# Moving the convolution, the fourth head's logits and the layer norm around TensorE's queue in a one-layer encoder block

## What is computed

```python
h = rms_norm(x, g_mix)
u_conv, q, k, v, qi, ki, wi, gc, ga = split(h @ w_in)
# conv branch
a, gate = split(u_conv, 2)
v = a * sigmoid(gate)                       # 512 channels
v = depthwise_causal_conv(v, 31 taps) + conv_b
y_conv = silu(layer_norm(v, ln_g, ln_b)) @ w_conv_out
# attention branch: 8 heads, 2 groups of keys, keys chosen by an indexer (top 128)
y_attn = softmax(q k / 8 + rel_bias, chosen keys only) v @ w_attn_out
x = x + (sigmoid(gc) * y_conv + sigmoid(ga) * y_attn) @ w_out
```

## Time and profile before

| | |
|---|---|
| runs | 720.65, 720.75, 723.16 us; median 720.75 |
| profiled execution | 723.9 us, span 722.1 us |
| mean granted TensorE clock | 0.91 |
| TensorE busy | 566.6 us (78%) |
| VectorE busy | 353.0 us (49%) |
| ScalarE busy | 258.5 us (36%) |
| POOL busy | 249.9 us (35%) |

### The profile page before, as it was taken

How to read it: one execution, slowest core, us unless ns; L and a number is a source line. 1 busy time by engine, 2 the same in 40 slices (tenths; PEclk the granted TensorE clock), 3 DMA queues, 4 the chain that set the end, 5 groups by cost and what they waited for, 6 DMA issues and landing times.

```text
span 722.1 us, 12345 instructions
## 1 busy us (share of the span) xinstructions
PE 566.6 (78%) x4247; PEld 377.3 (52%) x4250; DVE 353.0 (49%) x740; ACT 258.5 (36%) x443; POOL 249.9 (35%) x434
## 2 busy tenths in 40 slices
PE   3899999964979997989999903889988959696810
PEld 3577788742646564557788802445444524353400
DVE  4329999987887765186913282121212111111136
ACT  6344432312334465476431400323333322232312
POOL 5332444311212121124653005334453542434314
PEclk9999999985979999899999955999999999999965
DMA  8213532420120203023316698999999999999653
GB/s 281 62 60 94 199 93 83 117 58 0 59 59 1 58 1 117 10 108 116 106 41 233 224 414 331 380 408 407 361 347 408 409 408 408 408 403 398 242 224 130
DMA packets 58812, 149.21 MB, mean 207 GB/s; under 512 B 8660, under 2 KB 25044, under 8 KB 58782
## 3 DMA queue, kind: packets, MB, share of 16 engines
q1 hardware_dynamic: 53438, 139.89, 51.8%
q0 software_dynamic: 5200, 8.41, 3.2%
q10 hardware_dynamic: 144, 0.52, 0.2%
HBM read 145.37 MB, written 12.08 MB: 218 GB/s over the span
## 4 chain that ended last, share of the span: by engine, by line
PE 42%; DVE 28%; SPq 12%; issue 6%; DMA 6%; ACT 4%; POOL 1%; DVEq 1%; ACTq 0%; POOLq 0%
PE bank L650 20%; PE bank L871 9%; SPq L407 9%; DVE bank L1214 7%; PE bank L888 5%; DVE bm L1192 4%; DVE m L1191 4%; SPq L417 3%; DMA region<-in_w_e_up 2%; DVE conv_buf L1183 2%; PE bank L722 2%; PE bank L848 2%; PE bank L753 1%; ACT region L1015 1%; PE bank L819 1%
## 5 line engine op out<-in xcount | busy, mean ns | idle before, releaser
L524 POOL TENSOR_TENSOR w_part<-region,w_part 128x1024 fp32r<-128x1024 f32 (+1 forms) x52 | 110.1, 2117 | 246.5 <-ACT w_part L922 246.5
L650 PE MATMUL bank<-h_hi,w_part 128*128 128x512 f32 (+1 forms) x528 | 174.1, 405 | 3.2 <-DVE h_lo L1141 1.7
L650 PEld LDWEIGHTS bank<-h_hi,w_part 128*128 128x128 f32 (+1 forms) x528 | 100.7, 191 | 34.8 <-issue 9.1
L871 PE MATMUL bank<-region,kT 128*32 128x256 f32 x1536 | 93.5, 398 | 16.6 <-DMA region<-in_w_e_up 12.2
L650 PE MATMUL bank<-h_lo,w_part 128*128 128x512 f32 (+1 forms) x264 | 105.4, 399 | 0.0
L1477 DVE TENSOR_TENSOR mask_b<-mask_b,bank 128x128 f32<-128x128 f32 x30 | 8.6, 288 | 188.0 <-ACT mask_b L1100 117.8
L1214 DVE SCALAR_TENSOR_TENSOR bank<-glu,cv,bank 128x512 f32<-128x512 f32 x116 | 87.6, 755 | 19.0 <-DVE bank L1214 14.0
L871 PEld LDWEIGHTS bank<-region,kT 128*32 128x32 f32 x1536 | 56.0, 115 | 61.5 <-issue 39.1
L922 ACT ACTIVATE w_part<-region 128x1024 fp32r<-128x1024 f32 (+1 forms) x52 | 48.0, 924 | 107.2 <-PE bank L650 107.1
L550 POOL TENSOR_TENSOR carrier<-mhalf 128x1 f32<-128x1 f32 x184 | 32.9, 196 | 125.7 <-ACT qT L1104 117.0
L650 PEld LDWEIGHTS bank<-h_lo,w_part 128*128 128x128 f32 (+1 forms) x264 | 50.6, 192 | 11.0 <-issue 0.7
(11 more groups left out here) (252 smaller groups left out, 807.1 us busy)
## 6 DMA issues: line engine op xcount, KB each, us to landing
region<-in_w_e_down SPq DMA_DIRECT2D x22, 1024.0 KB
region<-in_w_e_gate SPq DMA_DIRECT2D x44, 512.0 KB
region<-in_w_e_up SPq DMA_DIRECT2D x44, 512.0 KB
region<-in_w_in SPq DMA_DIRECT2D x16, 1024.0 KB, 6.0
gates<-in_w_e_gate SPq DMA_DIRECT2D x20, 512.0 KB
gates<-in_w_e_up SPq DMA_DIRECT2D x20, 512.0 KB
conv_buf<-in_w_e_down SPq DMA_DIRECT2D x10, 1024.0 KB
region<-in_w_out SPq DMA_DIRECT2D x2, 2048.0 KB, 7.7
```

The lines of the kernel that those rows point to most:

```text
L524: g.tensor_tensor(unit_part(u, 1), unit_raw(u), unit_part(u, 0).bitcast(F32), ALU.subtract)\
L650: last = mm(out_, a_parts[p], b_parts[q], start=start and x_ == 0, stop=stop and x_ == 2)
L871: last = mm(bank[0][32 * c:32 * c + 32, 0:FF], xTs[:, k, at_:at_ + 32], w_gu[slot][:, e, :, half, k, j * P:(j + 1) * P], start=(half == 0 ...
```

## The change

It has four parts.
1. The convolution: each tap becomes two instructions of 256 columns, the two halves in turns; a half waits for the same half of the tap before. All 248 are written out, with no rolled loop. A table says how many taps stand where: first ahead of the reciprocal of a round, then between the logits of three heads and those of the fourth; 12 are left for behind the last round.
2. In each round the logits of the next round's fourth head move behind the value product on TensorE, and behind the second piece of taps on VectorE. The output copy of a round moves from the next round into its own.
3. The attention branch (units 33 to 40) moves ahead of the layer norm, of which the channel mean, the variance and the spreading stand between its units. `o_part` gets another layout, so that its first half can be written while the last round still uses its probabilities. Branch products use banks 2, 3, 4, 0.
4. The variance becomes one number per token (16 products with one column of ones), POOL raises it to the power -1/2 between two weight splits, VectorE scales an identity by it, and one product with ones spreads it over the partitions. The square root, the reciprocal and the correcting steps go.

```diff
-        o_part = part("o_part", [P, 2, CC, T], r0_at + 4 * 4096)
+        o_part = part("o_part", [P, CC, 2, T], r0_at + 4 * 4096).rearrange("p c u n -> p u c n")
...
             for u in range(NUNIT):
                 split_lo(u)
+                if u == AO0 + 5:
+                    pool.wait_ge(S["lnvar_ready"], 1)
+                    g.tensor_tensor(rs[:, 2, :], ss[:, 2, :], mhalf[:].to_broadcast([P, TB]), ALU.pow)\
+                        .then_inc(S["lnstd_ready"], 1)
...
                 project(units_a[i])
-                if i + 1 < len(attn):
-                    logits(i + 1, (3,))
...
                 last.then_inc(S["pv_mm"], 1)
-                if i == len(attn) - 1:
...
+                if i + 1 < len(attn):
+                    logits(i + 1, (3,))
                 if units_b[i]:
                     project(units_b[i])
...
+            def channel_variance():
+
+                pe.wait_ge(S["sq_ready"], CC)
+                for b in range(TB):
+                    for c in range(CC):
+                        last = mm(bank[7][:, b:b + 1], sT[:, c, b * P:(b + 1) * P], ones[:, 0:1],
+                                  start=(c == 0), stop=(c == CC - 1))
+                last.then_inc(S["ln_mm"], 1)
+
+            def spread_rstd():
+
+                pe.wait_ge(S["diag_ready"], 1)
+                mm(bank[7][:], ones[:], score, start=True, stop=True).then_inc(S["ln_mm"], 1)
...
             for u in range(AO0, CO0):
                 branch_out(u, o_part)
+                if u == AO0 + 3:
+                    channel_mean()
+                if u == AO0 + 4:
+                    channel_variance()
+                if u == AO0 + 5:
+                    spread_rstd()
...
+                if i >= len(attn) - 2:
+                    if i == len(attn) - 1:
+                        split_hi(NPROJ + 1)
+                    act.wait_ge(S["ot_ev"], i + 1)
+                    for c in range(2 * gr, 2 * gr + 2):
+                        a(o_part[:, 0, c, :], oT[:, c, :], ACT.Copy).then_inc(S["o_hi"], 1)
+            unit_out(NPROJ - 1)
...
+            def conv_half(n, hf):
+
+                c, j = divmod(n, TAPS)
+                cols = slice(hf * HALF, (hf + 1) * HALF)
+                shifted = glu[:, c, hf * HALF + j:(hf + 1) * HALF + j]
+                out_ = acc[:, cols] if j < TAPS - 1 else yv[:, c, cols]
+                if n:
+                    dve.wait_ge(S["conv_step"], 2 * n + hf - 1)
+                if j == 0:
+                    ins = v.tensor_scalar(out_, shifted, cv[:, c, 0:1], cv[:, c, TAPS:TAPS + 1], ALU.mult, ALU.add)
+                else:
+                    ins = v.scalar_tensor_tensor(out_, shifted, cv[:, c, j:j + 1], acc[:, cols], ALU.mult, ALU.add)
+                ins.then_inc(S["conv_step"], 1)
...
+            taps_at = ((7, 0), (10, 5), (4, 6), (10, 7), (6, 7), (12, 8), (8, 8), (0, 14))
+            taps_end = 12
...
+            logits_out(0, (0, 1, 2, 3))
             for i, (b, gr) in enumerate(attn):
-                conv_piece(6 if i == 2 else 4)
+                conv_piece(taps_at[i][0])
                 dve.wait_ge(S["ex_done"], i + 1)
                 v.reciprocal(ri[:, i % 2, :], sm[:, i % 2, :]).then_inc(S["ri_ready"], 1)
                 if i + 1 < len(attn):
-                    logits_out(i + 1)
-                if i:
-                    outputs_out(i - 1)
...
+                    logits_out(i + 1, (0, 1, 2))
+                conv_piece(taps_at[i][1])
+                if i + 1 < len(attn):
+                    logits_out(i + 1, (3,))
+                outputs_out(i)
+                if i >= len(attn) - 2:
+                    attn_low(attn[i][1])
+            conv_piece(taps_end)
```

More of the change, by code:

```diff
@@ L1245, in logits_out, with conv_piece @@
+            def conv_piece(taps):
+                for n in range(taps_done[0], taps_done[0] + taps):
+                    for hf in range(2):
+                        conv_half(n, hf)
+                taps_done[0] += taps
+            def logits_out(i, heads):
                 b, gr = attn[i]
```

128 lines of the change are left out of this document (47 added, 81 removed).

## The result

| | before | changed |
|---|---|---|
| median of 5 runs | 720.75 us | 730.65 us |
| lowest to highest | 720.1 to 723.16 | 729.69 to 733.83 |
| ratio, 95% interval | | 1.0142 (1.0123 to 1.0161) |
| profiled execution, span | 723.9, 722.1 us | 733.83, 730.4 us |
| mean granted clock | 0.91 | 0.91 |

The change makes the kernel 1.4% slower. The forecast was 716.5 us, and the time lies outside its range of 703 to 725.

A forecast was written before the change was run, and what follows sets the result against it. TensorE was taken to bound the kernel, idling mostly in one 12.4 us hole and slowed by the clock behind it. Attention -13.0 and tail +8.8 sum to -4.2: 720.75 - 4.2 = 716.5 us, range 703 to 725.

The forecast's parts named there:

- The taps: VectorE's convolution: a tap as two halves takes 0.80 us; unrolling saves about 15 us of VectorE's time, none on the path.
- The waits of the rounds: Attention: new TensorE waits of 2.8, 2.7, 4.2, 2.8 in rounds 1, 3, 5, 7, plus 2.1 for fourth logits: 14.6 us.
- The clock in the rounds: Attention: TensorE's clock falls three times, behind the waits of rounds 1, 3 and 5, at 3.3 us each: 10 us.
- The tail: From last value product to first conv product: 45.9 us with three waits of 2.6, 3.3 and 4.2; with clock +8.8 us.
- The clock in the tail: Behind the last value product: one of the three waits may bring a clock fall, +2 us (0 to 6).
- behind, all is shifted whole: From the conv products on: everything only moves in time, with no change in length, 0 us.
- The variance per token: Tail: its 32 one-column passes take TensorE 3.4 us, as much as the whole-width form, so nothing is won.
- The gain moves to the tail and every wait brings a fall: Rival: attention's gain is lost in the tail, clock falls of 13 and 6, +2.8 us, 723.5 us; chance 0.09.
- the clock holds: Rival: the short waits don't lower TensorE's clock, or taps are cheaper; -16.2 us, 704.5 us; chance 0.23.
- not for one of 1.7: Earlier trace: it agrees that the clock falls behind a wait of 2.8 us, but not behind one of 1.7 us.
- Halves wait each other out: Rival: each half tap starts only after the one before left the pipe; tap 0.98 to 1.06, 727 us; chance 0.13.
- the cause of the hole: TensorE's 12.4 us without a matmul: 10 turns of 3 taps stand on VectorE ahead of the second round's logits.

The follow-up runs named there:

- e1_taps: The kernel before with its taps alone changed: all written out in halves of 256 columns, same places and number; 712.26 us, ratio to before 0.9872.
- e5_keep2: The changed kernel with extra matmuls that nobody reads ahead of TensorE's waits, in the odd rounds and the tail; 716.06 us, ratio to before 0.9899.
- e6_table: e1_taps with the taps placed otherwise by a table, 12 left behind the last round, nothing else moved; 697.92 us, ratio to before 0.9643.
- e8_var: e1_taps with the variance per token alone, the order of the tail as in the kernel before; 717.40 us, ratio to before 0.9920.
- e3_tail: e1_taps with everything behind the last value product as in the changed kernel, no tap left for the end; 730.73 us, ratio to before 1.0120.
- e10_table2: e6_table with taps moved once more to where VectorE still waited for TensorE, 9 behind the last round; 694.07 us, ratio to before 0.9616.
- e11_odd: The changed kernel with its table of taps alone altered, fewer ahead of the odd rounds' reciprocals; 714.28 us, ratio to before 0.9880.
- e12_all: e11_odd with ScalarE's and VectorE's tail queues reordered and the first conv product waiting for quarters of s_part; 703.00 us, ratio to before 0.9748.

## Why the prediction was wrong, point by point

**The taps** (0.80 us, halving worth nothing): right, 0.79 in halves and 0.79 whole. Unrolling was put at 0.14 us a looped tap; in before they start 0.90 us apart in the first of the four tiles and 0.94 in the others, so it saves 0.11 to 0.15. That none of it is on the path by itself was wrong: e1_taps gains 1.3%, twice what I gave the whole change (4.2 us).

**The waits of the rounds.** Forecast 2.8, 2.7, 4.2, 2.8 in rounds 1, 3, 5, 7, and 2.1 for the fourth logits; measured 4.1, 3.0, 3.9, 3.0 and 2.1. Together 16.1 against 14.6. Only the first was mis-sized, by 1.3. The idle time in the rounds is 23.0 us against 5.7 + 14.6 = 20.3: 2.7 us of the miss; 1.1 of it are the transposes' waits for evicted ones (0.9 in before), which were in no term. The 1.3 us have a place as well: ahead of the copy and the taps of round 1 VectorE negates the maxima, 0.17 us in most rounds and 1.73 here, until a split of POOL's has ended:

```profile
158.03 2.34 POOL L528 TENSOR_TENSOR w_part<-region,w_part 128x1024 fp32r<-128x1024 f32 x1 [4.99 <-ACT w_part L948]
158.66 1.73 DVE L1271 TENSOR_SCALAR nm<-mx 128x4 f32<-128x4 f32 x1
```

**The clock** is the step that failed, in the rounds and more so in the tail: the sum had 12 us for it (10 and 2), and the runs showed 13.7 in the rounds and some 7.6 behind them (half of the 15.3 us of work at 0.50 there). Of this, e5_keep2 gave 15.9 back.

**The clock in the rounds.** I had four waits of 2.7 us or more in the sum and let the clock fall behind three: the one of round 7 was left out, though it was sized like the rest. Four falls at 3.4 us (13.7) came, where the sum had 10 for three of 3.3. With TensorE's work at full clock 0.4 us shorter than forecast, that makes up the other 3.3 us. The price of one fall was right, and the upper bound that I named, 13, was nearly the value.

**The tail.** The three waits were forecast as 2.6, 3.3 and 4.2 and measured as 3.3, 3.3 and 5.4; 2.0 of the miss. In the last one VectorE makes the last gate product, which had to wait for the last output product, and its four subtractions then take 4.64 us, not 2.7, beside two of POOL's splits:

```profile
336.54 0.69 DVE L1316 TENSOR_TENSOR gates<-gates,bank 128x512 f32<-128x512 f32 x1 [1.28 <-PE bank L658]
...
337.14 4.64 DVE L1335 TENSOR_TENSOR s_part<-conv_buf,s_part 128x512 fp32r<-128x512 f32 x4
337.74 3.49 POOL L528 TENSOR_TENSOR w_part<-region,w_part 128x512 fp32r<-128x512 f32 x2 [5.55 <-ACT w_part L948]
```

That was to be read from the kernel before, where the same four stand beside two splits of POOL's as well; the sum took the 0.68 of another instruction:

```profile
324.44 4.20 DVE L1310 TENSOR_TENSOR s_part<-conv_buf,s_part 128x512 fp32r<-128x512 f32 x4
```

**The clock in the tail** had 2 us for one fall "by one of the three waits". Three falls came: in the first output products (13.2 us for 11.2), in and behind the variance (4.5 for 3.6, then 5.35 for 2.8), and into the first conv products (2.3). TensorE's busy time from the last value product on rose by 6.0 us in the tail and 2.3 in the conv products, of which I had 0.6 and the 2. The terms were mis-sized by about 5.7 us, nearly all of it clock. Of the 2.3, "behind, all is shifted whole" was wrong: a wait at the end of a stretch charges the next stretch. Behind that it held, to 1.3 us.

**The variance per token** as "nothing won": right for TensorE's time (3.6 us at full clock against 3.6), but the fall behind it was in no term.

**The rivals.** "The gain moves to the tail and every wait brings a fall" had the mechanism, with a chance of 0.09, and even it reached only 723.5, since its clock in the tail was capped at 6 and its waits were mine. I had given the other side, that the clock holds, 0.23, on rows with waits of 1.1 and 1.7 us; the waits of the sum were twice that, and the row nearest to them, the 2.8 us in the earlier trace rows with its fall, spoke for every one of them falling. The list of falls was also short by one. Just ahead of the earlier trace rows TensorE waits 1.79 us in the kernel before (139.67 to 141.46 us), and the clock falls behind that wait too:

```profile
141.80:145.20 3.40, 3.40 (x9) 2.60 (x9) 2.51 (x6) 2.45 (x9) 1.46 (x1) 0.50 0.04 12
```

So "not for one of 1.7" held for one such wait of that trace and not for the other. "Halves wait each other out" is refuted by the 0.39 us between starts.

**Above all**, the forecast had the cause of the hole right, too many taps ahead of the second round's logits, and did not ask whether anything but their places had to change. e6_table removes the hole with a row of numbers and no matmul moved.

## What to carry to other kernels

When an engine off the path fills another's waits, place its work by what the other has to do in each round, and try that table before moving any matmul: it gave 2.6% here (0.9616 / 0.9872) on top of the 1.3% of the written-out taps, and the rearrangement itself nothing that could be found. Count each new wait of TensorE of about 3 us twice, once as itself and once as the clock behind it (3.4 us here), and count it for every wait in the sum, the last one before the next stretch too. It is no upper bound, since the clock also fell behind shorter waits. A form that makes an engine's chain shorter was worth nothing here, where what follows has less work left to hide it: the old layer norm had all eight output products over its chain, the new one two behind the spreading.

## What the runs showed of the hardware

- 32 fp32 passes of one column each, 3.6 us of TensorE without a gap, are followed by 3 to 6 us at a granted clock of 0.50 to 0.66, also where no wait of over 1.1 us stands around them (e8_var: 1.00 during the passes, 0.50 after a wait of 1.06 us; the same wait behind 8 passes of 512 columns left it at 1.00).
- The same wait can lower the clock or not. TensorE waited 2.71 us for the last round's probabilities in e1_taps and in e6_table; behind it the clock was 0.50 in the one and 1.00 in the other:

```profile
277.50:283.33 5.83, 5.14 (x24) 2.85 (x23) 0.00 (x0) 2.20 (x5) 1.27 (x1) 0.50 0.00 0
```

```profile
259.10:261.80 2.70, 1.80 (x14) 1.26 (x12) 2.70 (x8) 2.12 (x5) 0.00 (x0) 1.00 0.00 0
261.80:263.85 2.05, 1.95 (x16) 1.06 (x16) 2.05 (x6) 1.05 (x3) 1.28 (x1) 1.00 0.00 0
```

  What decides it was not found. The wait of 1.8 us ahead of the first round's fourth logits lowered it in before, the changed kernel, e6_table and five more, and not in e1_taps, e3_tail, e8_var, e10_table2 and e11_odd; e10_table2 has a fall behind 1.17 us, and e5_keep2 two behind waits of at most 0.8. So the gain of such a table varies from run to run: e10_table2's four lie between 690.9 and 698.0 us.
- Matmuls that nobody reads can hold the clock: they gained 2.4% (e5_keep2 against the changed kernel) though TensorE did more.
- Four subtractions of 512 columns on VectorE took 4.64 us beside POOL's splits (4.20 in before) and 2.50 without them for most of their time (e12_all). A VectorE instruction on 4 columns took 1.73 us instead of 0.17 and ended when POOL's split did, 160.4 us in the changed kernel.
